# Paged keys taken four pages to a matmul, scores stored by sequence, one more key slot, values loaded onto every fourth partition

## The chip, the core and the metric

The kernel runs on one core of one Trainium2 chip. Five engines work side by side: TensorE (PE, matmuls; its weight loads are listed as PEld), VectorE (DVE), ScalarE (ACT), GpSimd (POOL) and SyncE (SP). SP, POOL and ACT also start DMA transfers, each on a queue of its own, and 16 DMA engines carry them all. SBUF is the on-chip memory of 128 partitions, PSUM holds matmul results in 8 banks of 512 float32 columns. The metric is the device time of one execution in microseconds (us), lower is better.

## What is computed

A decoder step of two layers. 512 prompt tokens and 8 sample tokens (one for each of 8 sequences) go through the same weights. The part that the change touches is the attention of the 8 sample tokens over 4096 cached positions each, held in 32 pages of 128 positions that a page table names:

```python
def mla_sample_attn(q_nope, q_rope, ckv_new, kr_new, ckv_past, kr_past, w_uk, w_uv):
    q_lat = jnp.einsum('bthd,rhd->bthr', q_nope, w_uk)
    s_past = (jnp.einsum('bthr,bsr->bhts', q_lat, ckv_past)
              + jnp.einsum('bthd,bsd->bhts', q_rope, kr_past))
    s_new = (jnp.einsum('bthr,bsr->bhts', q_lat, ckv_new)
             + jnp.einsum('bthd,bsd->bhts', q_rope, kr_new))
    sc = jnp.concatenate([s_past, s_new], axis=-1).astype(jnp.float32) * scale
    pr = jax.nn.softmax(sc, axis=-1)
    o_lat = (jnp.einsum('bhts,bsr->bthr', pr[..., :npast], ckv_past)
             + jnp.einsum('bhts,bsr->bthr', pr[..., npast:], ckv_new))
    o = jnp.einsum('bthr,rhd->bthd', o_lat, w_uv)
```

With 8 heads, 256 latent and 32 rotary columns, a layer reads 256 pages of keys (a transposed copy with 288 columns for each of 128 partitions, 147 KB) and the same 256 pages as values (131 KB). Around it stand the projection `h @ w_in`, the prompt's own attention, a gating MLP, a gated linear attention, and a SwiGLU block, all as matmuls over 520 columns.

## The kernel before

Every weight matrix comes in slabs of 128 output columns (512 KB for 8 blocks of contraction). ACT starts the load and makes a rounded copy `wh`, DVE the rest `wl`, and PE runs three passes (lines 1921 to 1923: high by high, low by high, high by low) for each block and each half of 260 columns. `linear` does one slab: 48 matmuls. PE has one order, written out by hand; what it has to wait for are semaphores of the other engines and of the DMAs.

The sample attention is woven into that order. In each layer there is a **key stage** and then a **value stage**.

- Key stage. 8 pages (2 for each of 4 sequences) are a unit `w`, 32 units a layer. `keys(w)` waits for the unit's load, then takes for each of 4 sequences `bj` a stationary block of 32 query columns (`qlz`), out to 32 PSUM partitions of its own: 8 matmuls of 256 columns for the latent part (line 2177) and 16 of 64 columns for the rotary part (line 2182). Four of them, for four `bj`, run side by side in strips of 32 array columns. Each unit is put between the blocks ("steps") of 12 projection slabs, `KEY_FILLERS`: after 2 or 3 of the 8 steps of each. After the second slab stands `turn_values` (16 transposes), after the fourth `mix_tokens` (64 matmuls, line 2233, from the tile `vtok`). Every bank of 4 units is copied to `scs` by ACT and its maximum taken by DVE. Two sets of 8 head rows of a sequence group (`g`) share the 32 partitions, and of the 32 rows 16 are used.
- Key slots. Five slots: `kpg0` to `kpg2`, the pair `kx_most`/`kx_last`, and `ky`. SP loads the even units, POOL the odd ones, 8 DMAs each, in order. A queue waits until the unit that held the slot is read ("read K.."). Lines 2549 to 2572 (SP) and 2632 to 2643 (POOL).
- Between the stages. DVE makes the maximum of all, ACT the exponentials (line 1675, 8 pieces of 512 columns), PE turns each piece (`turn_scores`, four 128x128 transposes of `scs`) and DVE copies it to `pT`.
- Value stage. 64 value units `u` of 4 pages. `values(col)` waits for two units and does 8 matmuls of 256 columns (line 2207). Each round `c` of 8 has 8 units, a slab `P1c` (4 steps) and a slab `g1(c+1)` (8 steps). Eleven slots `vpg`, later nine; SP and POOL load them by turns, 4 DMAs each (lines 2579 and 2650), each partition taking 1 KB of a page.

## Time and profile before

| | us |
|---|---|
| median of 3 runs | 2041.92 (2040.01 to 2042.92) |
| the profiled execution, its own time | 2037.94 |
| its span in the trace | 2036.2 |
| PE busy | 2017.8 |
| key stage of layer 0 on PE | 173.1 to 302.4 |
| value stage of layer 0 on PE | 311 to 421 |

The profiled execution is 4.0 us below the median of the runs, and 1.7 us of its time lie outside the span. A profile's row of a matmul group is read as: start, length, engine, line, output from inputs, contraction rows * output columns, moving partitions x columns, how many. A float32 matmul is recorded as two instructions, so that `x16` at line 2177 is 8 matmuls. Matmuls overlap; what one costs is read from the starts around it and not from its length. The DMA share of a window is the busy share of the 16 DMA engines; it reads a little over 1 when they are full.

### The profile page before, as it was taken

How to read it: one execution, taken by the hardware profiler on the slowest of the kernel's cores; microseconds unless marked ns; L12 is line 12 of the kernel's file. 1: busy time of each engine (PE TensorE's matmuls, PEld its weight loads, DVE VectorE, ACT ScalarE, POOL GpSimd, SP SyncE). 2: the span in 40 equal slices, each digit the busy share in tenths (PEclk: the TensorE clock that was granted, in tenths of full speed). 3: DMA queues.
4: the chain of work that ended last, by engine and by line, in shares of the span. 5: the costliest groups of instructions: out<-in, count | busy, mean ns of one | idle time of the engine just before them, and what ended most of it. 6: DMA issues, size and time to landing. Idle time of an engine off the chain costs nothing.

```text
span 2036.2 us, 49885 instructions
## 1 busy us (share of the span) xinstructions
PE 2017.8 (99%) x21040; PEld 1915.6 (94%) x21040; DVE 1045.8 (51%) x1605; ACT 716.4 (35%) x1127; POOL 279.1 (14%) x520
## 2 busy tenths in 40 slices
PE   9999999999999999999999999999999999999998
PEld 9998888889999999999999988888999999999998
DVE  7876423366656444433367754234775654444333
ACT  5454114265333222222234531323653332222221
POOL 0003555600000000000000044565000000000000
PEclk9999999999999999999999999999999999999999
DMA  6427899942433333233353298999224333332332
GB/s 230 130 72 263 296 357 325 361 131 67 139 99 95 94 91 93 87 96 87 99 179 105 84 307 299 335 341 364 83 69 131 104 94 94 91 96 86 95 90 75
DMA packets 165557, 322.44 MB, mean 158 GB/s; under 512 B 24419, under 2 KB 104854, under 8 KB 164822
## 3 DMA queue, kind: packets, MB, share of 16 engines
q10 hardware_dynamic: 46944, 147.87, 23.5%
q1 hardware_dynamic: 93814, 100.04, 14.9%
q0 software_dynamic: 24576, 71.34, 10.1%
q8 instruction: 166, 2.72, 0.5%
q14 instruction: 57, 0.47, 0.1%
HBM read 307.08 MB, written 12.08 MB: 157 GB/s over the span
## 4 chain that ended last, share of the span: by engine, by line
PE 95%; DVE 2%; ACT 1%; DMA 1%; issue 0%; ACTq 0%; SPq 0%; DVEq 0%
PE PS L1921 28%; PE PS L1923 27%; PE PS L1922 27%; PE PS L2177 3%; PE PS L2207 3%; PE PS L1974 2%; PE PS L2182 1%; DMA vpg<-in_cache_vals 1%; PE PS L2233 0%; PE PS L2375 0%; PE PS L1960 0%; DVE wl L699 0%; PE PS L1981 0%; PE PS L2337 0%; DVE kxl L706 0%
## 5 line engine op out<-in xcount | busy, mean ns | idle before, releaser
L1921 PE MATMUL PS<-hh,wh 128*128 128x260 f32 x3008 | 862.6, 287 | 1.3 <-DVE gtmp L1104 1.0
L1923 PE MATMUL PS<-hl,wh 128*128 128x260 f32 x3008 | 850.6, 283 | 0.0
L1922 PE MATMUL PS<-hh,wl 128*128 128x260 f32 x3008 | 849.5, 282 | 0.0
L1921 PEld LDWEIGHTS PS<-hh,wh 128*128 128x128 f32 x3008 | 567.2, 189 | 14.9 <-issue 7.1
L1923 PEld LDWEIGHTS PS<-hl,wh 128*128 128x128 f32 x3008 | 567.4, 189 | 0.0
L1922 PEld LDWEIGHTS PS<-hh,wl 128*128 128x128 f32 x3008 | 567.0, 189 | 0.3
L699 DVE TENSOR_TENSOR wl<-raw,wh 128x1024 fp32r<-128x1024 f32 (+4 forms) x326 | 351.0, 1078 | 303.9 <-ACT wh L1455 302.9
L1455 ACT ACTIVATE wh<-raw 128x1024 fp32r<-128x1024 f32 (+4 forms) x326 | 304.3, 937 | 485.2 <-PE PS L1923 478.2
L1921 PE MATMUL PS<-fh,wh 128*128 128x260 f32 x704 | 199.3, 283 | 0.0
L1923 PE MATMUL PS<-fl,wh 128*128 128x260 f32 x704 | 198.7, 282 | 0.0
L1922 PE MATMUL PS<-fh,wl 128*128 128x260 f32 x704 | 198.6, 282 | 0.0
L2650 POOL DMA_DIRECT2D vpg<-in_cache_vals x256 | 137.4, 537 | 86.7 <-PE PS L2207 56.2
L1922 PEld LDWEIGHTS PS<-fh,wl 128*128 128x128 f32 x704 | 132.6, 188 | 0.1
L1923 PEld LDWEIGHTS PS<-fl,wh 128*128 128x128 f32 x704 | 132.6, 188 | 0.0
L1921 PEld LDWEIGHTS PS<-fh,wh 128*128 128x128 f32 x704 | 132.4, 188 | 0.1
L1654 ACT ACTIVATE gsig<-gsig 128x520 f32<-128x520 f32 x48 | 30.6, 638 | 221.0 <-DVE gsig L1095 220.9
L1388 DVE TENSOR_TENSOR fsig<-PS,rs 128x520 f32<-128x520 f32 x44 | 30.8, 700 | 135.5 <-PE PS L1923 135.3
L2622 POOL DMA_DIRECT2D kx_most<-in_cache_keys x14 | 7.6, 546 | 654.4 <-issue 653.5
L1879 ACT ACTIVATE fsig<-fsig 128x520 f32<-128x520 f32 x44 | 28.2, 640 | 196.3 <-DVE fsig L1388 196.2
L2641 POOL DMA_DIRECT2D kpg<-in_cache_keys x112 | 60.1, 537 | 268.4 <-issue 214.8
L1095 DVE TENSOR_TENSOR gsig<-PS,rs 128x520 f32<-128x520 f32 x48 | 33.6, 699 | 122.1 <-PE PS L1923 121.1
L1923 PE MATMUL PS<-ml,wh 128*128 128x260 f32 x256 | 72.3, 283 | 0.0
(362 smaller groups left out, 2989.5 us busy)
## 6 DMA issues: line engine op xcount, KB each, us to landing
raw<-in_wpack ACTq DMA_DIRECT2D x238, 512.0 KB, 3.6
vpg<-in_cache_vals SPq DMA_DIRECT2D x256, 128.0 KB, 6.1
vpg<-in_cache_vals POOLq DMA_DIRECT2D x256, 128.0 KB, 5.4
kpg<-in_cache_keys SPq DMA_DIRECT2D x224, 144.0 KB, 4.5
kpg<-in_cache_keys POOLq DMA_DIRECT2D x112, 144.0 KB, 4.8
ky<-in_cache_keys POOLq DMA_DIRECT2D x96, 144.0 KB, 4.1
raw<-in_wpack ACTq DMA_DIRECT2D x48, 256.0 KB, 2.9
raw<-in_wpack ACTq DMA_DIRECT2D x16, 384.0 KB, 3.1
```

Source lines behind the costliest of these rows:

```text
L699: dve.tensor_tensor(wl[s][:, 0:n], raw[s][:, 0:n], wh[k % W_RING][:, 0:n].bitcast(F32), ALU.subtract).then_inc(*mark("w_low_ready", f"wlo ...
L1095: dve.tensor_tensor(halves(gsig[m % 2][:, :]), pair(f"g{j}{m}"), halves(rs[:, :]), ALU.mult).then_inc(*mark("gate_scaled", f"gate {j}{m}"))
L1388: dve.tensor_tensor(halves(fsig[f % 2][:, :]), pair(f"gt{f}"), halves(rs[:, :]), ALU.mult).then_inc(*mark("gate_scaled", f"scaled {f}"))
L1455: act.activation(wh[k % W_RING][:, 0:n], raw[k % RAW_RING][:, 0:n], ACT.Copy).then_inc(*mark("w_high_ready", f"whi {k}"))
L1921: pe.matmul(out, w[0], x[0], start=first, stop=False)
L1922: pe.matmul(out, w[1], x[0], start=False, stop=False)
L1923: return pe.matmul(out, w[0], x[1], start=False, stop=last)
L1974: return pe.transpose(out, in_, ident[0:n, 0:n])
L2177: ins = pe.matmul(out[32 * bj:32 * bj + 32, q, :], qlz[:, kk, 120 * g + 32 * bj:120 * g + 32 * bj + 32], pages[:, :, PAGE * kk:PAGE * kk + ...
L2207: ins = pe.matmul(bank("O")[r, 256 * g:256 * g + 256], pT[c % 2][:, col % 4, r], vpg[VALUE_SLOT[u]][:, bj, :], start=False, stop=u == 63)
L2641: pool.dma_start(key_page(w, bj, q), a["cache_keys"][bass.ds(l, 1), bass.ds(numbers[4 * q + bj], 1), :, :].rearrange("a n p c -> p (a n c) ...
L2650: pool.dma_start(vpg[VALUE_SLOT[u]][:, bj, :], a["cache_vals"][bass.ds(l, 1), bass.ds(numbers[4 * q + bj], 1), :, :].rearrange("a n p r -> ...
```

## The change

The pages' positions are dealt out otherwise. In the host's copy of the keys, position `4t+j` of a page stands at column `32j+t` of the latent part, and the rotary part is stacked the same way on 4 groups of 32 partitions. A query block now sits in rows `8j..8j+7` of the 32 output rows, with zeros around it, so that position class `j` lands in its own rows: `latent_query(kk, b, j)` is a window of 32 columns moved by 8 for each `j`. All 32 rows of a sequence are used, the rotary part needs one matmul instead of four (`qrz`), and scores are stored by sequence, block and head.

- Two units of one sequence group are taken together in 16 blocks `b` (`KEY_STEP` puts one after every 6 or 7 steps). Where their two slots form one of three `KEY_PAIRS`, one matmul covers 4 pages, 4 x 32 columns: 36 matmuls of 128 columns for two units. Blocks 4 to 15 are such pairs. In blocks 0 to 3 each unit has its own 36 matmuls of 64 columns. Out goes to PSUM with the 32 positions 4 float32 apart.
- Slots: 0, 1, 2, 4, 5, 6 in pairs (1,2), (0,4), (6,5), and slot 3 once. Slot 6 lies over `vtok` and waits for "pe mx3", the end of `mix_tokens`; slot 5 waits for "pe o7".
- `scs` is half as wide (2048 columns in all): 4 pieces to turn instead of 8. The maximum and the sum now have to be taken over four groups of rows as well (`over_blocks`: five small DVE instructions, each waiting for the one before).
- Values: a page goes onto partitions `page, page+4, ...` of a slot, 32 partitions with 4 KB each instead of 128 with 1 KB. A group is 4 slots, waited for together, then 16 matmuls of 256 columns with 8 stationary columns each. 13 slots, later 11.
- The new tokens' part has four matmuls more, `Ot` two transposes more, and tiles of the linear attention (`S1`, `zz`, `ATd`, `hv1`, `hr1`) lie elsewhere; DVE's `head_variances` waits for "out S1 1".

```diff
-KEY_SLOT = [4, 3, 0, 1, 2, 4, 0, 3, 1, 2, 4, 3] + [0, 1, 2, 4] * 5
+KEY_STEP = {round(6.4 * b) - 1: b for b in range(1, 16)}
+KEY_BANKS = ((0, 2), (2, 6), (6, 10), (10, 14), (14, 16))
+KEY_SLOT = [4, 3, 0, 1, 2, 0, 4, 5] + [1, 0, 2, 4, 6, 1, 5, 2, 0, 6, 4, 5, 1, 0, 2, 4, 6, 1, 5, 2, 0, 6, 4, 5]
+KEY_PAIRS = ((1, 2), (0, 4), (6, 5))
...
-                            for q, pages in key_pages(w, bj):
-                                ins = pe.matmul(out[32 * bj:32 * bj + 32, q, :], qlz[:, kk, 120 * g + 32 * bj:120 * g + 32 * bj + 32],
-                                                pages[:, :, PAGE * kk:PAGE * kk + PAGE], start=(g, kk) == (0, 0), stop=False)
...
+                    out = bank(f"K{n}")[:, at:at + 128].rearrange("p (t i q) -> p i q t", i=2, q=2)
+                    blocks = [(kk, j) for kk in range(2) for j in range(4)] + [(2, 0)]
...
+                        for w in units:
+                            pe.wait_ge(*upto(f"keys {w}"))
+                        for kk, j in blocks:
+                            x = slice(PAGE * kk + 32 * j, PAGE * kk + 32 * j + 32)
+                            for bj in range(4):
+                                ins = pe.matmul(out[32 * bj:32 * bj + 32, :, :, :], stationary(kk, j, bj), key_pair[slots][:, :, bj, :, x],
+                                                start=(kk, j) == (0, 0), stop=kk == 2)
...
+                def over_blocks(src, op):
+                    dve.tensor_reduce(by_row[:, 0:2], src, AX.X, op).then_inc(*mark("dve_step"))
...
+                    dve.transpose(turned_rows[:, :], by_row[:, :]).then_inc(*mark("dve_step"))
...
+                    dve.tensor_reduce(best[:, :], turned_rows[:, :].rearrange("p (j h) -> p h j", j=4), AX.X, op).then_inc(*mark("dve_step"))
...
+                    dve.tensor_copy(spread[:, :, :], best[:, :].unsqueeze(1).broadcast_to([128, 4, 8])).then_inc(*mark("dve_step"))
...
+                    dve.transpose(by_row[:, :], spread[:, :, :].rearrange("p j h -> p (j h)")).then_inc(*mark("dve_step"))
...
+                    elif KEY_SLOT[w] == 6:
+                        sp.wait_ge(*upto("pe mx3"))
...
-                            sp.dma_start(vpg[VALUE_SLOT[u]][:, bj, :],
-                                         a["cache_vals"][bass.ds(l, 1), bass.ds(numbers[4 * q + bj], 1), :, :].rearrange("a n p r -> p (a n r)")).then_inc(
+                            for page in range(4):
+                                sp.dma_start(vpg[VALUE_SLOT[u]][page:128:4, :, :].rearrange("t j r -> t (j r)"),
+                                             a["cache_vals"][bass.ds(l, 1), bass.ds(numbers[page // 2][2 * (page % 2) + bj], 1), :, :].rearrange("a n (t j) r -> t (a n j r)", j=4)).then_inc(
```

On PE, the first key unit behind `mix_tokens` of layer 0, before (`kpg_141` is slot 0; rows between are the slab's passes):

```order
L2233 MATMUL PS<-wsT,vtok 64x128 x7
L1921 MATMUL PS<-hh,wh_63 128x260 [waits w_low_ready,dve_evac]
...
L1923 MATMUL PS<-hl,wh_63 128x260
L2177 MATMUL PS<-kpg_141,qlz 32x256 [waits keys_loaded0,act_evac]
L2177 MATMUL PS<-kpg_141,qlz 32x256 x7
L2182 MATMUL PS<-kpg_141,qlz 32x2x32 x16
L1921 MATMUL PS<-hh,wh_63 128x260
```

and with the change (`kp_215` are slots 0 and 4, `kp_216` slots 6 and 5):

```order
L2243 MATMUL PS<-kp_215,qlz 32x4x32 [waits keys_too_loaded4,keys_too_loaded0]
L2243 MATMUL PS<-kp_215,qlz 32x4x32 x31
L2243 MATMUL PS<-kp_215,qrz 32x4x32 x4
L2311 MATMUL PS<-wsT,vtok 64x128 [waits dve_evac,value_ready]
...
L2311 MATMUL PS<-wsT,vtok 64x128 x7
L1975 MATMUL PS<-hh,wh_63 128x260 [waits w_low_ready,dve_evac]
...
L1977 MATMUL PS<-hl,wh_63 128x260
L2243 MATMUL PS<-kp_216,qlz 32x4x32 [waits keys_loaded5,keys_loaded6,low_ready]
L2243 MATMUL PS<-kp_216,qlz 32x4x32 x31
L2243 MATMUL PS<-kp_216,qrz 32x4x32 x4
```

24 matmuls for one unit, behind 8 steps, became 36 for two units, behind 6 steps, and they wait for both loads, into slots 6 and 5.

On SP, the same unit pair's loads, units 12 and 14, before (`kpg0_141` slot 0; between the shown rows of a unit stand its other DMAs):

```order
L2572 DMA out_new_gmlp_v_sample<-xT_49 512x1x8 [waits value_ready]
L680 TENSOR_LOAD ptab_79
L2567 ISA [waits keys_read]
L2567 DMA kpg0_141<-in_cache_keys 128x288
...
L680 TENSOR_LOAD ptab_79
L2567 ISA [waits keys_read]
L2567 DMA kpg2_143<-in_cache_keys 128x288
```

and with the change:

```order
L2654 DMA out_new_gmlp_v_sample<-xT_49 512x1x8 [waits value_ready]
L706 TENSOR_LOAD ptab_79
L2649 ISA [waits group_ready]
L2649 DMA kp65_216<-in_cache_keys 128x288
...
L706 TENSOR_LOAD ptab_79
L2649 ISA [waits keys_read]
L2649 DMA kp65_216<-in_cache_keys 128x288
```

The wait ahead of unit 12 is no longer for a key unit that PE has read but for a group of PE, which is "pe mx3"; the loads of unit 14 and all later even units are queued behind it.

## Rows read from the trace of the kernel before

**Rows 1.** The page: busy time by engine, and the DMA share in 40 slices.
```profile
PE 2017.8 (99%) x21040; PEld 1915.6 (94%) x21040; DVE 1045.8 (51%) x1605; ACT 716.4 (35%) x1127; POOL 279.1 (14%) x520
...
DMA  6427899942433333233353298999224333332332
```

**Rows 2.** Busy time of windows of layer 0; last PE clock, DMA share, GB/s.
```profile
200.00:210.00 10.00, 10.00 (x166) 9.26 (x165) 5.87 (x8) 1.66 (x2) 4.29 (x8) 1.00 1.05 349
...
220.00:230.00 10.00, 10.00 (x144) 9.25 (x141) 9.51 (x17) 2.64 (x4) 1.51 (x3) 1.00 0.53 189
...
250.00:260.00 10.00, 10.00 (x189) 8.28 (x188) 2.61 (x3) 1.66 (x2) 5.83 (x12) 1.00 1.06 369
...
310.00:320.00 10.00, 10.00 (x114) 6.87 (x114) 2.28 (x3) 9.91 (x19) 4.49 (x9) 1.00 0.67 225
...
330.00:340.00 10.00, 10.00 (x112) 8.42 (x114) 3.17 (x4) 1.57 (x2) 6.45 (x12) 1.00 1.06 390
...
400.00:410.00 10.00, 8.03 (x84) 6.71 (x80) 4.23 (x9) 3.47 (x4) 4.30 (x9) 1.00 1.05 369
```

**Rows 3.** Timeline of PE around one key unit of layer 0.
```profile
180.66 0.28 PE L1923 MATMUL PS<-hl,wh 128*128 128x260 f32 x1
180.87 1.07 PE L2177 MATMUL PS<-kpg,qlz 128*32 128x256 f32 x16
181.76 0.63 PE L2182 MATMUL PS<-kpg,qlz 128*32 128x64 f32 x32
182.32 0.39 PE L1921 MATMUL PS<-hh,wh 128*128 128x260 f32 x1
182.55 0.28 PE L1922 MATMUL PS<-hh,wl 128*128 128x260 f32 x1
```

**Rows 4.** Groups of PE by line and shape: count, busy us, mean ns, idle before.
```profile
L2207 PE MATMUL PS<-vpg,pT 128*32 128x256 f32 x1024 | 62.7, 382 | 2.2 <-DMA vpg<-in_cache_vals 2.2
L2177 PE MATMUL PS<-kpg,qlz 128*32 128x256 f32 x672 | 45.0, 385 | 0.0
...
L2182 PE MATMUL PS<-kpg,qlz 128*32 128x64 f32 x1344 | 26.5, 219 | 0.0
...
L1974 PE MATMUL PS<-ident,scs 128*128 128x128 f32 x64 | 9.7, 274 | 0.0
```

**Rows 5.** Timeline of PE at the end of the value stage of layer 0.
```profile
399.81 1.07 PE L2207 MATMUL PS<-vpg,pT 128*32 128x256 f32 x16 [0.18 <-DMA vpg<-in_cache_vals]
...
409.79 1.07 PE L2207 MATMUL PS<-vpg,pT 128*32 128x256 f32 x16 [1.97 <-DMA vpg<-in_cache_vals]
```

**Rows 6.** Key loads: a unit's issue on SP and POOL, SP's waits, landing (150 to 215).
```profile
182.59 3.95 SPq L2567 DMA_DIRECT2D kpg<-in_cache_keys  x8
...
191.38 4.66 POOL L2641 DMA_DIRECT2D kpg<-in_cache_keys  x8 [5.29 <-PE PS L2182]
...
SPq L2567 <- PE PS L2182: 94.6, 22, 12.2
...
DMA to landing us min/median/max: 3.1/5.1/8.1
```

**Rows 7.** The chain that ended last: `mix_tokens`, start, length, line.
```profile
219.14 4.47 PE PS L2233 x64
```

**Rows 8.** Timeline between the stages of layer 0: maximum, exponentials, first turned piece.
```profile
303.14 0.69 DVE L1034 TENSOR_REDUCE mxs<-scs 128x1 f32<-128x512 f32 x1 [10.18 <-ACT scs L1649]
...
304.54 0.16 DVE L1086 TENSOR_REDUCE nms<-mxs 128x1 f32<-128x9 f32 x1
...
306.72 0.71 ACT L1675 ACTIVATE scs<-scs,nms 128x512 f32<-128x512 f32 x1
...
308.43 0.60 PE L1974 MATMUL PS<-ident,scs 128*128 128x128 f32 x4
```

**Rows 9.** Windows of 2 us in which the granted clock of TensorE fell.
```profile
168.00:170.00 2.00, 2.00 (x10) 2.00 (x9) 1.85 (x8) 0.00 (x0) 0.00 (x0) 0.50 1.03 319
...
1448.00:1450.00 2.00, 2.00 (x12) 1.93 (x11) 1.97 (x7) 0.27 (x1) 0.00 (x0) 0.50 0.37 115
```

More of the change, by code:

```diff
@@ L2236, in mix_tokens @@
                         ins.then_inc(*mark("group_ready", f"pe mx{i}"))
-                for unit in range(KEYS_FIRST):
-                    keys(unit)
+                keys(0)
                 pv(7)
```

382 lines of the change are left out of this document (222 added, 160 removed).

## The prediction, made before the changed kernel was run

> **What bounds the kernel now.** I read the page first: PE is busy for 2017.8 of 2036.2 us [rows 1], so time is lost or won where PE's own work or a wait of PE changes, and DVE (51%) and ACT (35%) matter only where PE waits for them. The DMA share by slices [rows 1] is the second thing to see: it is 2 to 4 tenths nearly everywhere, but 7 to 9 in two stretches of five slices, which are the key and value stages of the two layers. The windows of layer 0 make this sharp [rows 2]: from 180 to 410 us the 16 DMA engines are full (share 1.05, 349 to 390 GB/s), except for three dips, of which the deepest is 220 to 230 (0.53), where PE does `mix_tokens` and frees no key slot, and another is 310 to 320 (0.67). PE is not idle there, but the loads are only just in time: at the end of the value stage PE waits 0.18 and 1.97 us for a value load [rows 5]. SP for its part waits 94.6 us in 22 waits for PE to read key units [rows 6]. So in these stages PE and the DMA engines run at nearly the same pace. If PE gets faster there, the loads become the limit. The expected gain has to be taken as the smaller of two differences.
>
> **Part 1, key matmuls (less PE work).** A unit of before [rows 3]: PE's last pass ahead of it starts at 180.66, the second behind it at 182.55. Without the unit that would take 2 x 0.12 us (the distance of passes), so a unit costs 1.65 us; 0.89 us are the 16 records of 256 columns, 0.56 us the 32 records of 64 columns, 0.2 us the change of shape on both sides. 32 units are 52.8 us a layer. By columns: four records side by side take 222 ns for 256 columns and 70 ns for 64. The changed pair has 72 records of 128 columns, 18 groups of four. Half of 222 ns is 111 ns; from the short shape up, 70 ns plus 64 columns at 222/256 ns is 126 ns. I take 117, so 2.1 us and with the 0.2 us 2.3 us for two units. The 8 units of blocks 0 to 3 have 72 records of 64 columns: 18 x 70 ns = 1.26 us each. Sum: 12 x 2.3 + 8 x 1.26 + 4 x 0.2 + 0.3 for the split slot 3 = 38.8 us. This is **14.0 us less a layer**, all of it on PE's path.
>
> No matmul of before writes PSUM with gaps; the changed ones put neighbouring positions 4 float32 apart. So the price of 117 ns has no row behind this side. Bounds: no effect below (a write can't become faster by gaps), and above twice the group's time, that is, each gapped record of 128 columns costing what 256 columns cost without gaps (222 ns). I take no effect, since a group of four with 256 columns needs 222 ns, or 0.87 ns for one column, about two periods of a 2.4 GHz clock, so that a write has two periods already.
> The Trainium skill speaks against this change here: its page "Advanced Engine Details and Errata", section "PSUM Cachelines", says that PSUM has cachelines of 8 bytes and that any non-contiguous access pattern slows matmuls significantly. No row of before can show it. By that rule the gain of part 1 turns into a loss, which is rival B below.
>
> **Part 2, fewer turns.** 64 transposes of `scs` in both layers cost about 0.6 us for four [rows 4, 8], 4 groups a layer go: 2.4 us. Against it stand one more transpose of `sn8`, two of `Oacc` and four matmuls of 256 columns, 0.8 us together. **1.6 us less a layer.** The values' matmuls keep their number and columns, 512 a layer at 62.7 us of 1024 records in all [rows 4]; 8 stationary columns instead of 32 I cost at nothing (their strips of 32 are the same; bounds minus 1 us a layer, if a part of the 9 ns above the plain column time is weight load, and nothing above).
>
> Parts 1 and 2: 15.6 us of PE work less in each layer.
>
> **Part 3, the wait of block 6 (new).** Units 12 and 14 go to slots 6 and 5, and unit 12 waits for "pe mx3". Before, 5 slots cycled and the load of unit 12 waited only for an earlier unit. Now SP can start it when `mix_tokens` ends (219.14 + 4.47 = 223.6 us in before [rows 7]). SP needs 3.95 us for 8 DMAs [rows 6], twice plus 0.3 us for page numbers, and a DMA takes at least 3.1 us from its issue to landing [rows 6]: the second unit is there 0.3 + 3.95 + 0.35 + 3.6 + 3.1 = 11.1 us after mx3 (the last DMA is issued 0.4 us before the end). Block 6 stands 6 steps (6 x 0.717 = 4.3 us) behind `mix_tokens`. **PE waits 6.5 us, in each layer.** All of PE's order is behind it, and on SP the loads of all later even units are queued behind the "mx3" wait. This wait can't be hidden, since nothing on PE stands between. POOL has units 13, 15 and 17 issued by then, but its unit 19 waits for slot 6.
>
> **Part 4, loads behind block 6.** A pair takes 6.4 steps (4.6 us) and 2.3 us, 6.9 us. In that time 2 x 1.18 MB of keys and 0.8 of a slab (0.42 MB) have to come: 403 GB/s, against 349 to 369 in full windows of the key stage [rows 2]. At 355 GB/s a pair needs 7.8 us. From block 6 to block 15 there are 9 periods, 8.4 us of waits if nothing is loaded ahead; 3 units are, and by bytes alone (15 units and 7 slabs, 21.4 MB, 60.3 us, plus 3 us landing, against 62.3 us of PE) 1 us is left. Between 1 and 8.4: going through the stage unit by unit with these lengths, slots and the two queues, I get 5.8 us at 355 GB/s and 4.9 at 360. The same tally for before has no wait in the key stage, 1.0 us in the value stage, and its end at 421.6, where the trace shows 421. **I take 5.5 us a layer.** In the value stage, PE's round needs 4.98 MB in about 13 us in both kernels; 13 slots and later 11 instead of 11 and 9 cover it, so the 2.2 us of layer 0 [rows 5] go.
>
> **Part 5, small things between the stages.** Maximum, `nms` and exponentials end just ahead of PE: the first piece is done at 307.5 and turned at 308.43 [rows 8], 0.9 us of cover. `over_blocks` adds four dependent instructions of 0.19 us on DVE, ACT has two pieces for each one (plus 0.9 us), the last bank is half as wide (minus 0.6): 1.1 to 1.2 us, so 0.3 us on PE a layer. The `over_blocks` behind the value stage runs while PE turns the values and does D0 and D1 (3 us), at nothing. `head_variances` waits for a store that is some 30 us old.
>
> **Part 6, value loads.** Same bytes and number of DMAs, 4 KB rows instead of 1 KB. Rows of 4 KB (the weight slabs) and of 1 KB run mixed in the full windows, so no row tells their rates apart; bounds 340 to 410 around the 355 to 390 there [rows 2]. Faster than now gives nothing (part 4), so I take the present rate.
>
> **Sum.** A layer: -15.6 + 6.5 + 5.5 + 0.3 = -3.3 us; two layers -6.6, less the 2.2 of rows 5: -8.8. A fall of TensorE's clock during the new 6.5 us wait is likely in one layer or the other: at 0.50, that is 1.2 GHz, PE started 10 or 12 matmuls in 2 us [rows 9] where the passes' distance of 0.12 us gives 17; such a window loses 0.7 us or so and its neighbours a part more. Ahead of it PE had run small matmuls only. I add 1.5. Total -7.3 us: the profiled execution 2037.94 becomes 2030.6, the median 2041.92 becomes **2034.5**.
>
> **The rivals.**
> A, the loads keep up. For: in the windows at 250 and 330, 369 and 390 GB/s were moved. Then part 4 gives nothing back and only block 6 is waited for: 2 x (-15.6 + 6.5 + 0.3) - 2.2 = -19.8, about **2022**.
> B, slower: PSUM writes with gaps double a group. It decides once a group of 128 columns takes more than about 150 ns. At 213 ns a pair costs 4.0 us, an alone unit 1.95: 65.2 us against 52.8, +12.4 a layer, -1.6, +6.5 for block 6, +0.3, part 4 gone, -2.2 once: +33, **2075**. Against it: the two periods for a column, above. The skill's rule speaks for it.
> C, slower: rows on every fourth partition come in worse, 320 GB/s in the value stage. A round then needs 15.6 us against 13; with 13 slots ahead, 6 rounds wait, about 11 us a layer: -8.8 + 22 + 1.5, **2056**. Against: the four loads of a slot cover all partitions together.
> D, no change: the change does its work, but the waits take it all (355 GB/s turns out 345, part 4 8 us; both block-6 waits drop the clock): -15.6 + 7 + 8 + 0.3 is -0.3 a layer, -2.2, +3: **2041**.
> That the matmuls with 8 stationary columns would not run four side by side (the change not doing what it says) would be over +80 us a layer; every float32 strip of 32 in before does, so 1%.
>
> **How the numbers follow.** Forecast 0.41, A 0.15, B 0.14, C 0.08, D 0.21, the last 0.01. A measurement here tells 0.2%, 4 us, from no change. Faster by more: A, and most (0.35) of the forecast: 0.50. Same: the rest of it and most of D: 0.24. Slower: B, C, the last, some of D: 0.26. The range reaches from below A (2017) to beyond C (2060), leaving out B and the best end of A.
>
> **What would show it.** Key matmuls: line 2243 groups, four records 117 ns apart (right) or over 150 (B). Part 3: PE idle some 6.5 us, released by a key DMA, once a layer behind `mix_tokens`, DMA share low there. Part 4: waits of 1 to 2 us for key loads at blocks 10 to 15 with DMA share near 1.05; none would be A. Part 6: value-stage GB/s of 355 or more, no waits at value groups. Wrong altogether if PE waits for DVE or ACT between the stages by more than 1 us.

## The result, and the profile of the changed kernel

The changed kernel takes 2059.51 us, median of 4 runs (2055.8 to 2060.82), against 2041.34 for the kernel before on the same chip: a ratio of 1.0087, 95% interval 1.0073 to 1.0100. It is **slower**, by 18 us. The forecast was 2034.5 and faster; the range of 2017 to 2060 holds the time, near its upper end. The profiled execution is 2055.8 us against 2037.94, its span 2054.1 against 2036.2, so the two traces differ by 17.9 us.

The page answers [rows 1]: PE's busy time, and the DMA share in 40 slices.

```profile
span 2054.1 us, 49473 instructions
...
PE 1998.5 (97%) x20802; PEld 1915.3 (93%) x20802; DVE 1039.3 (51%) x1611; ACT 709.6 (35%) x1125; POOL 274.1 (13%) x520
...
DMA  6427899942432323333353289999324323333332
```

PE is busy for 19.3 us less than before, and its idle time grew from 18.4 to 55.6 us. What PE waited for (line, releaser, us in total, times, longest):

```profile
PE PS L2243 <- DMA kp<-in_cache_keys: 26.1, 6, 8.7
PE PS L2253 <- issue: 9.8, 3, 4.4
```

L2243 is a key pair, L2253 an unpaired key unit. The waits of [rows 5] for values have no line any more. The groups that answer [rows 4]:

```profile
L2284 PE MATMUL PS<-vpg,pT 128*8 128x256 f32 x1024 | 61.2, 380 | 0.0
L2243 PE MATMUL PS<-kp,qlz 128*32 128x128 f32 x1536 | 53.7, 298 | 26.3 <-DMA kp<-in_cache_keys 26.1
...
L2028 PE MATMUL PS<-ident,scs 128*128 128x128 f32 x32 | 4.9, 276 | 0.0
```

The timeline of PE in layer 0, key stage and after, tells where the time went (start, length, operation, idle time ahead and its releaser; it answers [rows 3], [rows 7] and [rows 8]):

```profile
173.67 1.10 PE L2253 MATMUL PS<-kp,qlz 128*32 128x64 f32 x64
...
191.72 1.08 PE L2253 MATMUL PS<-kp,qlz 128*32 128x64 f32 x64
197.20 0.44 PE L2253 MATMUL PS<-kp,qrz 128*32 128x64 f32 x8 [4.41 <-issue]
...
221.38 1.96 PE L2243 MATMUL PS<-kp,qlz 128*32 128x128 f32 x64 [1.44 <-DMA kp<-in_cache_keys]
...
223.48 4.54 PE L2311 MATMUL PS<-wsT,vtok 128*64 128x128 f32 x64
...
241.18 3.64 PE L2243 MATMUL PS<-kp,qlz 128*32 128x128 f32 x64 [8.66 <-DMA kp<-in_cache_keys]
244.56 0.68 PE L2243 MATMUL PS<-kp,qrz 128*32 128x128 f32 x8
...
275.72 3.64 PE L2243 MATMUL PS<-kp,qlz 128*32 128x128 f32 x64 [4.09 <-DMA kp<-in_cache_keys]
...
314.27 0.40 PE L2243 MATMUL PS<-kp,qrz 128*32 128x128 f32 x8
...
320.77 0.60 PE L2028 MATMUL PS<-ident,scs 128*128 128x128 f32 x4
...
325.48 1.91 PE L2284 MATMUL PS<-vpg,pT 128*8 128x256 f32 x32
...
432.79 0.66 PE L2028 MATMUL PS<-ident,Oacc 128*128 128x128 f32 x4
```

Three things can be seen. Block 6 (241.18) waits as foretold, and longer; block 10 (275.72) waits too. The wait at 197.20 is one that the prediction had not: it stands **inside** a unit, ahead of its last 8 records, where the program has no wait at all. And the same 64 records that take 1.96 us at 221.38 take 3.64 behind the long waits, since TensorE's granted clock had fallen to 0.50, that is 1.2 of 2.4 GHz. The windows show both that and the DMA engines (PE, PEld, DVE, ACT, POOL, granted clock, DMA share, GB/s), against [rows 2] and [rows 9]:

```profile
200.00:210.00 10.00, 10.00 (x203) 9.77 (x203) 4.19 (x4) 1.59 (x2) 2.09 (x4) 0.89 0.29 81
...
240.00:250.00 10.00, 8.82 (x107) 8.47 (x108) 1.93 (x2) 1.06 (x1) 3.47 (x7) 0.67 0.92 268
...
340.00:350.00 10.00, 10.00 (x102) 8.77 (x99) 2.83 (x5) 1.24 (x2) 7.38 (x15) 1.00 1.02 398
...
238.00:240.00 2.00, 0.00 (x0) 0.00 (x0) 0.00 (x0) 0.00 (x0) 0.00 (x0) 0.50 0.83 245
244.00:246.00 2.00, 2.00 (x28) 1.62 (x21) 0.00 (x0) 0.00 (x0) 0.09 (x1) 0.50 0.83 240
```

From 200 to 210 the share was 1.05 before [rows 2]; now it is 0.29, with PE at work all the time. The queues say why. GpSimd's queue, SyncE's queue, and what SyncE's waited for in this layer (they answer [rows 6]):

```profile
182.23 4.97 POOL L2726 DMA_DIRECT2D kp<-in_cache_keys  x8 [0.66 <-issue]
207.76 2.30 POOL L2726 DMA_DIRECT2D kp<-in_cache_keys  x4 [20.56 <-PE PS L2253]
```
```profile
185.72 11.89 SPq L2649 DMA_DIRECT2D kp<-in_cache_keys  x16
197.66 0.60 SPq L2654 DMA_DIRECT2D out_new_gmlp_v_sample<-xT  x1
228.20 42.29 SPq L2649 DMA_DIRECT2D kp<-in_cache_keys  x53
```
```profile
SPq L2649 <- PE PS L2311: 29.2, 1, 29.2
```

GpSimd's queue stood 20.6 us with unit 9, whose slot 0 still held unit 5 (read only in block 3, at 207), though slot 4, for unit 11 behind it, was free from 197.6 on. SyncE's stood 29.2 us with unit 12, for the end of `mix_tokens` at 228.0, though slot 5 for unit 14 was free from block 3 on.

Time from start to start, in both traces. The key stage runs from its first to the end of its last key matmul, the value stage from its first value matmul (325.48) to the first transpose of `Oacc` (432.79). Half clock is the busy time of PE in windows of 1 us, times what the granted clock there lacks to 1.

| | predicted, a layer | layer 0 | layer 1 |
|---|---|---|---|
| key stage before | | 173.1 to 302.4, 129.3 | 1180.7 to 1310.1, 129.4 |
| key stage after | | 173.7 to 314.7, 141.0 | 1188.8 to 1328.1, 139.3 |
| of it: waits inside units | 0 | 4.4 | 5.4 |
| of it: wait of block 5 | 0 | 1.4 | 1.3 |
| of it: wait of block 6 | 6.5 | 8.7 | 7.6 |
| of it: waits behind block 6 | 5.5 | 4.1 | 3.1 |
| of it: half clock | 1.5 in both | 7.6 | 7.2 |
| the rest, PE's own work | -14.0 | 114.8, so -14.5 | 114.8, so -14.6 |
| between the stages | +0.3 | +0.6 | +0.6 |
| value stage | -1.6, and -2.2 once | 112.3 to 107.3, -5.0 | 109.7 to 107.3, -2.4 |

Unrounded, the sums are +7.2 and +8.1 us; the other 2.6 of the 17.9 us lie outside these stages. Over the whole program half clock takes 18.0 us in this trace and 5.1 in the trace of before, 12.9 us more. PE's longer idle time (+37.2) and its shorter work apart from the clock (-32.2) leave the other 5.0.

### The profile page after: what moved, and what is told of

The parts are those of the page before. It is cut to its first block, busy times and chain, and to the rows that moved or that the text cites. A ratio compares the mean times of both kernels' runs of the same rounds, so it can differ in the third digit from the quotient of the medians.

```text
span 2054.1 us, 49473 instructions
## 1 busy us (share of the span) xinstructions
PE 1998.5 (97%) x20802; PEld 1915.3 (93%) x20802; DVE 1039.3 (51%) x1611; ACT 709.6 (35%) x1125; POOL 274.1 (13%) x520
## 3 DMA queue, kind: packets, MB, share of 16 engines
q8 instruction: 164, 2.69, 0.5%
## 4 chain that ended last, share of the span: by engine, by line
PE 90%; DMA 3%; issue 2%; SPq 2%; DVE 2%; ACT 1%; POOLq 0%; ACTq 0%; POOL 0%; DVEq 0%
PE PS L1975 27%; PE PS L1977 26%; PE PS L1976 26%; PE PS L2284 3%; DMA kp<-in_cache_keys 2%; PE PS L2243 2%; SPq L2649 2%; PE PS L2028 2%; PE PS L2253 1%; PE PS L2311 0%; PE PS L2415 0%; PE PS L2453 0%; PE PS L2014 0%; DMA xT<-in_x_t 0%; PE PS L2035 0%
## 5 line engine op out<-in xcount | busy, mean ns | idle before, releaser
L2726 POOL DMA_DIRECT2D kp<-in_cache_keys x240 | 129.7, 540 | 362.1 <-issue 232.7
L2736 POOL DMA_DIRECT2D vpg<-in_cache_vals x256 | 131.8, 515 | 88.5 <-PE PS L2284 50.3
L2243 PE MATMUL PS<-kp,qlz 128*32 128x128 f32 x1536 | 53.7, 298 | 26.3 <-DMA kp<-in_cache_keys 26.1
```

The source lines that it names most:

```text
L2243: ins = pe.matmul(out[32 * bj:32 * bj + 32, :, :, :], stationary(kk, j, bj), key_pair[slots][:, :, bj, :, x], start=(kk, j) == (0, 0), sto ...
L2726: pool.dma_start(key_page(w, bj, q), a["cache_keys"][bass.ds(l, 1), bass.ds(numbers[number_of(bj, q)], 1), :, :].rearrange("a n p c -> p ( ...
L2736: pool.dma_start(vpg[VALUE_SLOT[u]][page:128:4, :, :].rearrange("t j r -> t (j r)"), a["cache_vals"][bass.ds(l, 1), bass.ds(numbers[page / ...
```

## The experiments

All times are medians, each beside runs of the kernel before on the same chip (2038.8 to 2041.7 us). The changed kernel's variants scatter more than the kernel before (2045.6 to 2058.0 in e5, 2031.3 to 2056.3 in e14), so a difference between two of them is clear only where their intervals lie apart. The changed kernel's own is 1.0073 to 1.0100. The theory at the start: what is lost is waits for key loads, and the half clock behind them, on PE's path. The first question was what makes the loads late: the slot behind `mix_tokens`, the order of the queues, or the rate of the DMA engines (called L below).

**Block 6 in free slots.**

```diff
-KEY_SLOT = [...] + [1, 0, 2, 4, 6, 1, 5, 2, 0, 6, 4, 5, ...
+KEY_SLOT = [...] + [1, 0, 2, 4, 1, 0, 2, 4, 6, 0, 5, 4, ...
```


> One edit of the changed kernel: block 6 takes slots 1 and 2 (free when block 4 is read), block 7 slots 0 and 4, block 8 slots 6 and 5, block 9 slots 0 and 4. No load ahead of block 6 waits for mix_tokens any more. Theory W (the wait at block 6 is the slot over vtok, with the half clock behind it): the idle time of 8.7 and 7.6 us at block 6 goes or falls under 2 us, and with it the half clock of some 5 us behind it (2.2 us of work lost); loads run on through mix_tokens, so the wait of 4.1 and 3.1 us at block 10 shrinks too. Per layer 7 + 2.2 + 2, so 2059.5 - 22 = about 2037. Rival L (the DMA engines' rate sets the end of the stage): the wait only moves from block 6 to blocks 8 to 13, total of waits falls by no more than 3 us a layer, 2050 to 2057.

Measured 2061.54, ratio 1.0107 (1.009 to 1.0124), no gain. Block 6 waited no more, but PE waited for keys 25.2 us in 8 waits. Block 5 waited longer, 3.1 and 4.2 us in place of 1.4 and 1.3. The longest waits stand at block 9, which takes slots 0 and 4 two blocks after block 7 had them, and has to wait until they are read and loaded:

```profile
261.95 3.64 PE L2243 MATMUL PS<-kp,qlz 128*32 128x128 f32 x64 [5.13 <-DMA kp<-in_cache_keys]
```

So the wait of block 6 can't be taken away by itself. As a test between slots and rate it was poor, since the edit made a new slot shortage.

**Work that keeps PE busy while it waits.**

```diff
                     if b == first:
                         begin(f"K{n}")
+                        for i in range({6: 18, 10: 6}.get(b, 0)):
+                            for bj in range(4):
+                                pe.matmul(bank(f"K{n}")[32 * bj:32 * bj + 32, 0:256], latent_query(0, bj, 0), qlz[:, 0, 0:256], start=True, stop=True)
```
The first run had 36 and 14 in place of 18 and 6.

> The changed kernel with matmuls that do nothing needed ahead of block 6 (36 groups of four with 256 columns, some 8 us at full clock) and ahead of block 10 (14 groups, some 3 us), written into the bank that the block then overwrites. PE would have been idle there. It prices TensorE's clock by itself. Theory C (the half clock behind each wait costs its 2.2 to 2.5 us of work and PE's time is the path): granted clock stays at 1.00 behind blocks 6 and 10, the waits are as long as the filler leaves, and the time falls by 2 x (2.2 + 2.3) = 9 us, to 2050.5; less where the filler itself runs over the end of the wait. Rival L (loads set the pace): what the clock gives is waited for at the next blocks, within 2 us of 2059.5.

Measured 2069.14, ratio 1.0151 (1.0132 to 1.0169): the filler was twice as long as meant, 15.6 us, and block 6 came at 246.8 in place of 241.2. It tells nothing of the clock's price. The second run was sized by it:

> The filler again, half as long: 18 groups (144 records) ahead of block 6 and 6 groups ahead of block 10. In the run before, 288 records took 15.6 us, 54 ns each, and PE came to block 6 at 246.8 in place of 241.2: I had counted a matmul as one record, it is two. Now 7.8 and 2.6 us. Theory C (half clock costs its 2.3 us behind each wait, on the path): clock 1.00 behind blocks 6 and 10, key stage ends 4 us earlier in each layer, 2059.5 - 8 = 2051. Rival L (loads set the pace): the waits at blocks 10 and 15 grow by what the clock gives, within 3 us of 2059.5.

Measured 2055.91, ratio 1.0075 (1.0058 to 1.0092): 3.6 us less than the changed kernel, where theory C said 8 and L said 3 or less. The intervals overlap, so these 3.6 us are not clear. The clock stayed at 1.00 behind blocks 6 and 10 of both layers, but blocks 8 and 14 of layer 0 then waited 2.7 and 2.1 us and block 8 of layer 1 3.2 us; block 14 ran at half clock, and that block 8 in part:

```profile
255.24 1.96 PE L2246 MATMUL PS<-kp,qlz 128*32 128x128 f32 x64 [2.69 <-DMA kp<-in_cache_keys]
...
301.87 3.43 PE L2246 MATMUL PS<-kp,qlz 128*32 128x128 f32 x64 [2.14 <-DMA kp<-in_cache_keys]
```

The falls of the clock only moved: the half clock of both layers, from 140 to 480 and from 1150 to 1500, adds up to 17.5 us here and to 18.0 in the changed kernel. Two of the falls in this trace (315 to 320 and 1332 to 1337) have no wait for a load near them. So the run doesn't price the clock by itself, and keeping it up at single waits brought nothing back here.

**PSUM without gaps**, the price that no row of before could show.

```diff
-out = bank(f"K{n}")[:, at:at + 128].rearrange("p (t i q) -> p i q t", i=2, q=2)
+out = bank(f"K{n}")[:, at:at + 128].rearrange("p (i q t) -> p i q t", i=2, q=2)
```


> The key matmuls of the changed kernel write their 32 positions side by side in PSUM (no gaps of 4 float32) in place of one in four; the scores then stand in another order than the values' turning expects, nothing else changes. Theory (gaps cost nothing): a pair's 64 latent records stay at 1.95 us (111 ns for a group of four), the unpaired ones at 1.10, and the time is the same within 0.2%. Rival (gaps slow the write): the 64 records fall below 1.7 us and the time by 2 x 12 x 0.3 = 7 us or more.

Measured 2057.12, ratio 1.0087 (1.0067 to 1.0107), the same as the changed kernel's. The 64 records at full clock take as long as with gaps (1.96 above):

```profile
247.92 1.95 PE L2243 MATMUL PS<-kp,qlz 128*32 128x128 f32 x64
```

Rival B is out.

**Small key loads, in the changed kernel and in the kernel before.**

```diff
-sp.dma_start(key_page(w, bj, q),
+sp.dma_start(key_page(w, bj, q)[:, 0:KCOL if KEY_HOLDER[w] is None else 72],
```
and likewise for the source and for GpSimd's loads.

> The changed kernel with the same number of key DMAs, but only the first load of each slot is whole; later ones bring 72 of the 288 columns, a quarter of the bytes (scores of later units are then partly those of earlier ones). It takes the DMA engines' rate out and leaves queues, slots, landing and PE's work. Theory (rate and slots together): waits at blocks 5, 10 and the waits inside units without a semaphore (4.4, 3.0, 2.4 us, when a 16 KB block of PE's instructions came in beside full DMA engines) go, block 6 still waits, some 4 to 7 us with its half clock, since its loads start at the end of mix_tokens: 2059.5 - 38 - 15 + 2 x 8 = about 2022. If the waits inside units stay at 3 to 4 us, they have nothing to do with the load of the DMA engines: 2032. Rival (PE's work has not shrunk as read): over 2040.

Measured 2031.36, ratio 0.9956 (0.994 to 0.9971), 28 us less than the changed kernel (37 expected). Its waits:

```profile
PE PS L2243 <- DMA kp<-in_cache_keys: 14.1, 4, 6.9
PE PS L2253 <- issue: 2.7, 2, 1.4
```

Block 6 still waits 6.9 and 6.3 us, as a load behind `mix_tokens` must; the waits inside units fell from 9.8 to 2.7 us (two of 1.4 and 1.3), with the same instructions at the same places.

> The kernel before with later key loads of 72 of 288 columns (scores of later units are then partly those of earlier ones), as in e4 for the changed kernel, which fell by 28 us. Theory: the kernel before waits for no key load, so it stays within 3 us of its time, 2038 to 2041. Rival (full DMA engines slow something else too, such as PE's instructions or its matmuls): below 2033.

Measured 2040.87, ratio 1.0004 (0.9992 to 1.0017), as the theory said: small loads by themselves made that kernel no faster.

**Two unpaired units apart**, against the waits inside units.

```diff
-                keys(0)
+                keys(0, 0)
                 pv(7)
+                keys(0, 1)
...
+                        if KEY_STEP.get(8 * n + k - 2, 9) < 4:
+                            keys(KEY_STEP[8 * n + k - 2], 1)
```


> The changed kernel with the two unpaired units of blocks 0 to 3 apart: the second unit of block 0 behind the prompt's last matmuls, those of blocks 1 to 3 two steps after the first. Same matmuls, same loads. Theory I (a block of two unpaired units is 144 records and as many weight loads, 288 instructions in 2 us, and PE's next 16 KB of instructions comes in late beside full DMA engines): the waits of 3 to 4.4 us inside a unit, where the program has no wait, go or fall under 1.5 us, with the half clock behind them; 2059.5 - 2 x (3.5 + 2) = 2048 if nothing is waited for later, 2055 if half of it is. Rival U (it is the key load of the unit, put down wrongly): the waits stay, at the start of the second unit, 2058 to 2061.

Measured 2050.24, ratio 1.0064 (1.0039 to 1.0089): 9.3 us less than the changed kernel by the medians, though the intervals overlap. The trace decides: no wait inside a unit is left; the lines of PE's waits for keys and of its longest wait under "issue" are

```profile
PE PS L2243 <- DMA kp<-in_cache_keys: 29.0, 6, 8.6
PE PS L2423 <- issue: 1.2, 1, 1.2
```

(29.0 with the keys where it was 26.1: a part was given back at block 10.) So U falls. What these waits are can be seen in the DMA queues of the changed kernel:

```profile
q8 instruction: 164, 2.69, 0.5%
```

164 transfers of 16 KB are 2.69 MB. Their number follows PE's records: 154 for 19468 matmul records and as many weight loads in e12 and e15, 166 for 21040 in the kernel before, 171 for 21602 in e2, always 253 or 254 instructions of PE to a transfer. So this is PE's program coming in. In the stretch 194 to 196, just ahead of the end of the wait at 197.20, one such transfer is listed, while key loads held 99% of the engines:

```profile
q1 hardware_dynamic: 658, 0.67, 99.2%
q8 instruction: 1, 0.02, 3.5%
```

The waits of layer 1 look the same:

```profile
1193.76 0.32 PE L2253 MATMUL PS<-kp,qlz 128*32 128x64 f32 x8 [2.98 <-issue]
1214.20 0.48 PE L2253 MATMUL PS<-kp,qlz 128*32 128x64 f32 x19 [2.44 <-issue]
```

Windows of 0.1 us place the transfers that belong to the three waits at 194.6, 1191.1 and 1211.8; PE goes on 2.6, 2.7 and 2.4 us later. That distance is the same wherever such a wait occurs: in all 33 waits of this kind, 0.7 to 4.4 us long, in twelve traces of the changed kernel and its variants, PE goes on 2.3 to 2.7 us after one transfer on this queue has started, also in e4 (2.5 and 2.7), where the waits are short. Blocks of two unpaired units are 288 instructions in 2 us, more than one transfer brings. The Trainium skill, "Runtime: NRT & Kernel Launch", section "Instruction fetch mechanics", has it that an engine's instructions come in blocks of 16 KB, 256 instructions, while it works, and that this is mostly hidden; the size agrees with the trace, the hiding doesn't hold here. The runs show when the wait goes (units apart) or shrinks (small loads), and the fixed distance from the transfer speaks strongly for the instruction supply as the cause; why the transfer starts late beside full DMA engines is not shown. In e7, e10, e11, e14 and e16, whose units are apart too, waits of 0.7 to 2.9 us inside a unit came back, so apart is not enough by itself.

**The order of the queues.**

```diff
-KEY_SLOT = [4, 3, 0, 1, 2, 0, 4, 5]
+KEY_SLOT = [4, 3, 0, 1, 2, 3, 4, 5]
...
-                for w in range(3, 32, 2):
+                for w in (3, 9, 7, 5, *range(11, 32, 2)):
...
-                for i in range(16):
+                for i in (*range(6), 7, 6, *range(8, 16)):
```


> The changed kernel with other orders on the two load queues: unit 5 goes to slot 3 (read once before, then empty), unit 9 is loaded ahead of 7 and 5 into slot 0, and unit 14 (slot 5) ahead of unit 12 (slot 6, behind mix_tokens). Theory Q (queues that stand for a slot while others are empty cost the time: GpSimd's queue stood 20.6 us, SyncE's 29.2 us in layer 0, and the DMA share fell to 0.29 from 200 to 210): the share at 200 to 240 rises to over 0.95, the wait at block 6 falls from 8.7 to 4 to 5 us (one unit behind mix_tokens in place of two), block 5 waits no more, block 10 waits under 2 us. Per layer 4 + 1.4 + 2 and one half clock less (2.3): 2059.5 - 19 = about 2040. Rival L (rate): less than 6 us in all, over 2053.

Measured 2051.21, ratio 1.0054 (1.0035 to 1.0073): 8.3 us less, between Q (19) and L (under 6). Waits for key loads fell from 26.1 to 11.9 us, but 5.4 us more of block 6 are listed under "issue" (it starts 7.3 us behind the end of `mix_tokens`, with unit 12's load), and the waits inside units stayed (9.9 us). The share from 200 to 210 rose from 0.29 to 0.69, not to 0.95.

> Both edits together. Theory: they add up where neither hides the other, 2059.5 - 19 - 8 = 2032, below the kernel before. If the loads' rate is the limit, it comes out as the better of the two, not lower.

Measured 2046.83, ratio 1.0028 (1.0013 to 1.0044): 12.7 us less than the changed kernel, better than either by the medians, but not the 27 of the sum. Block 8 now waits 4.0 and 6.4 us, for units 16 and 18.

Two more orders on that line missed. Unit 16 ahead of unit 12:

```diff
-                for i in (*range(6), 7, 6, *range(8, 16)):
+                for i in (*range(6), 7, 8, 6, *range(9, 16)):
```


> As e7, and unit 16 is loaded ahead of unit 12 as well (SyncE's queue: 10, 14, 16, 12, 18). In e7 block 8 waited 4.0 and 6.4 us for units 16 and 18, queued behind the load of unit 12 that waits for mix_tokens. Theory Q: unit 18 is issued 4 us earlier, the wait of block 8 falls to 0 to 2.5 us and its half clock goes in one layer at least: 2046.8 - 2 x 4 = 2039. Rival L (rate): half of it or less, 2043 or more.

Measured 2048.35, ratio 1.0046 (1.0026 to 1.0067). Block 6 itself waited 5.6 us in both layers in place of 3.2 and 2.6, with unit 16's load issued ahead of its own; block 8 waited no more. And other steps besides:

```diff
-KEY_STEP = {round(6.4 * b) - 1: b for b in range(1, 16)}
+KEY_STEP = {s: b + 1 for b, s in enumerate((4, 10, 17, 24, 30, 40, 46, 52, 58, 64, 71, 77, 83, 89, 95))}
```


> As e10, with the blocks at other steps: 1 to 5 after steps 4, 10, 17, 24, 30 (one or two steps earlier, slots come free sooner), block 6 after step 40 in place of 37 (2.2 us later, unit 12 lands some 7.4 us behind mix_tokens), the rest every 6 or 7 steps. Theory: the hole in the DMA share from 200 to 240 gets smaller, block 6 waits under 1.5 us, 3 to 5 us less than e10 in all, about 2036. Rival L: the rate sets it, same as e10 within 2 us.

Measured 2051.39, ratio 1.0063 (1.0039 to 1.0086), 15 us above the theory; block 6 waited 3.7 and 3.4 us, block 10 of layer 0 5.8. Both results spoke for L, that the rate is the limit, until e12 and e15 below.

**Without waits: PE's own work.** e4, e1 and e5 together.

> The changed kernel with nothing to wait for in the key stage as far as that can be had: later key loads bring 72 of 288 columns (as in e4; scores of later units are then partly those of earlier ones), block 6 takes free slots (as in e1), unpaired units stand apart (as in e5). It measures the term of the sum by itself: PE's work. Theory (parts 1 and 2 of the prediction right, 15.6 us a layer): 2041 - 31 = 2010, a little less since the unpaired units took 1.03 us in place of 1.26 (8 x 0.2 x 2 = 3): 2005 to 2012, waits under 3 us a layer. Rival (the gain was never there, the traces' waits only show it): over 2025.

Measured 2020.78, ratio 0.9905 (0.9876 to 0.9934): 20 us below the kernel before, where 31 were expected. The key stage of layer 0 runs from 174.0 to 293.5, 119.5 us with 2.7 us of waits, so 12.5 us of work less; units apart may cost some of the 14.5, with more changes of shape.

**One part alone, in the kernel before: two units at once.**

```diff
-KEY_STEPS = [(2, 5, 7) if n % 2 == 1 else (3, 7) for n in range(len(KEY_FILLERS))]
+PAIR_AT = [round(6.4 * b) - 1 for b in range(1, 16)]
+KEY_STEPS = [tuple(s % 8 for s in PAIR_AT if s // 8 == n for _ in range(2)) for n in range(len(KEY_FILLERS))]
...
                             keys(KEY_START[n] + KEY_STEPS[n].index(k))
+                            keys(KEY_START[n] + KEY_STEPS[n].index(k) + 1)
```


> The kernel before with one part of the change alone: two key units at once after every 6 or 7 steps (the changed kernel's places) in place of one after 2 or 3 steps; its own matmuls, slots and value stage. Theory G (taking two units at once frees slots in pairs and later, so that the load queues stand and the DMA engines have holes): PE waits for key loads, 3 to 8 us a layer, 2047 to 2060. Rival (the grain does nothing, only the faster PE and slot 6 do): within 3 us of 2040.

Measured 2035.87 (10 runs), ratio 0.9978 (0.9968 to 0.9987). Theory G falls, on the other side: this is **faster** than the kernel before, with one wait of 0.5 us for keys. The timeline shows what is won. Two units and the pass behind them:

```profile
190.48 0.28 PE L1924 MATMUL PS<-hl,wh 128*128 128x260 f32 x1
190.70 1.07 PE L2178 MATMUL PS<-kpg,qlz 128*32 128x256 f32 x16
191.58 0.63 PE L2183 MATMUL PS<-kpg,qlz 128*32 128x64 f32 x32
192.03 1.05 PE L2178 MATMUL PS<-ky,qlz 128*32 128x256 f32 x16
192.89 0.63 PE L2183 MATMUL PS<-ky,qlz 128*32 128x64 f32 x32
193.45 0.39 PE L1922 MATMUL PS<-hh,wh 128*128 128x260 f32 x1
193.68 0.29 PE L1923 MATMUL PS<-hh,wl 128*128 128x260 f32 x1
```

From 190.48 to 193.68 less two passes of 0.12 us are 2.96 us for two units, against 2 x 1.65 by [rows 3]: one change of shape less. The key stage of layer 0 is 173.5 to 298.6, 4.2 us shorter.

**Is it the pace?** The kernel before with three of four rotary matmuls left out, unit by unit, then two at once:

```diff
-                    for t in range(4):
+                    for t in range(1):
```


> The kernel before with three of four rotary key matmuls left out (8 of 24 instructions' groups stay: scores lack part of the rotary product). PE's work in the key stage shrinks by 24 records of 64 columns a unit, 0.42 us, 13.4 us a layer: about what the change takes away, but with one unit at a time, the slots of before and no load behind mix_tokens. Theory L (the loads of the key stage stand so near PE's pace that any faster PE runs into them): the DMA share of that stage was 0.95, so some 6 us a layer are to be had and the rest turns into waits with half clock behind them; 2041 - 2 x 7 = 2027. Rival S (only the slots and order of the change spoil it): all of it shows, 2014. Rival N: nothing is to be had at all, over 2036.

Measured 2025.55, ratio 0.9924 (0.9903 to 0.9945), close to the value of L; but I had sized the removed work too large. By the distance of unit to unit it is 0.3 to 0.35 us a unit, some 10 us a layer, and of these the key stages got 9.0 and 9.9 us shorter (173.9 to 294.2 in layer 0, 120.3 us). PE waited little for keys:

```profile
PE PS L2177 <- DMA kpg<-in_cache_keys: 2.4, 2, 1.7
```

The DMA engines were full where the changed kernel's stood (200 to 210: share 1.06, 374 GB/s). So in the key stages nearly all of the work saved shows, as S has it. The whole program got less of it, 14.6 us by the medians and 11.4 in the profiled execution: that trace has 11.7 us of half clock in five places, none behind a wait for keys, against 5.1 in the trace of before. Why the clock fell there is open.

> The kernel before with two units at once (e9, its key stage 125 us) and without three of four rotary matmuls (e12, 120 us): with both PE's key stage is about 115 us, the pace of the changed kernel, with five slots, unit by unit releases and no load behind mix_tokens. Theory S: waits up to 4 us a layer, 2035.9 - 15 + 3 = about 2024 or less. Rival L: PE waits 6 us or more a layer with half clock behind it, key stage no shorter than the 120 us of e12, 2028 or more.

Measured 2023.56, ratio 0.992 (0.9902 to 0.9938). The key stages are 118.3 and 117.3 us, with 5.9 us of waits for keys in both layers together, so PE goes nearly at the changed kernel's own pace (114.8):

```profile
200.00:210.00 10.00, 10.00 (x125) 9.04 (x117) 4.96 (x7) 1.66 (x2) 6.46 (x12) 1.00 1.07 381
210.00:220.00 10.00, 10.00 (x147) 9.31 (x146) 4.84 (x8) 2.19 (x3) 6.47 (x12) 1.00 1.07 362
```

So the load engines do feed nearly this pace, from five slots in the order of before.

**The changed kernel with a cycle of three slot pairs**, on top of e7: units apart, unit 5 in slot 3 and unit 9 early are in it too, besides what is shown, and the waits of the value slots follow their new order.

```diff
-KEY_SLOT = [...] + [1, 0, 2, 4, 6, 1, 5, 2, 0, 6, 4, 5, 1, 0, 2, 4, 6, 1, 5, 2, 0, 6, 4, 5]
+KEY_SLOT = [...] + [1, 0, 2, 4, 1, 0, 2, 4, 6, 1, 5, 2, 0, 6, 4, 5, 1, 0, 2, 4, 6, 1, 5, 2]
...
-FIRST_SLOTS, LATER_SLOTS = (4, 5, 6, 1, 2, 3, 11, 12, 10, 9, 7, 8, 0), (4, 5, 6, 1, 2, 3, 11, 12, 7, 8, 0)
+FIRST_SLOTS, LATER_SLOTS = (1, 2, 11, 12, 8, 9, 10, 3, 4, 5, 6, 7, 0), (2, 11, 12, 8, 1, 3, 4, 5, 6, 7, 0)
...
-                for i in range(16):
+                for i in (*range(6), 9, 6, 7, 8, *range(10, 16)):
```


> The changed kernel with its load order set anew: unpaired units apart (e5), unit 5 in slot 3 and unit 9 early (e6), and from block 4 on the slot pairs (1,2), (0,4), then (1,2), (0,4), (6,5), (1,2), (0,4), (6,5) and so on, so that block 6 needs no load behind mix_tokens (as in e1) and no pair is taken again sooner than three blocks later, but for blocks 6 and 7 (in e1 block 9 was, and waited 5.1 us); unit 18 goes to slot 5 ahead of unit 12. The value slots are taken in the order in which the key slots now come free. Theory S (slots and order of the change spoil it, since in e12 the same load engines fed a key stage of 120 us with waits of 1 to 2 us): waits of the key stage under 5 us a layer and one half clock at most, key stage 120 to 125 us, 2059.5 - 2 x 16 = about 2027. Rival L (the last 5 us of pace are more than the loads can do): key stage 130 or more as in e7 and e10, 2043 to 2048.

Measured 2042.13 (10 runs), ratio 1.0002 (0.9978 to 1.0027): level with the kernel before, 17.4 us less than the changed kernel. The key stages are 127.6 and 131.4 us, more than the 120 to 125 expected, with waits of 8.6 and 11.4 us. The last run put the queues right for the units that were late there:

```diff
-                for w in (3, 9, 7, 5, *range(11, 32, 2)):
+                for w in (3, 7, 5, 9, 11, 18, *range(13, 32, 2)):
...
-                for i in (*range(6), 9, 6, 7, 8, *range(10, 16)):
+                for i in (*range(9), *range(10, 16)):
```


> As e14, with the early loads in another order: GpSimd's queue takes units 3, 7, 5, 9, 11, 18 and then 13 on (unit 5 is no longer behind 9: block 3 waited 2.0 and 2.3 us for it), and unit 18 moves from SyncE's queue to GpSimd's, which stood 18.9 us for unit 13's slot while SyncE was behind with units 20 and 22 (block 10 waited 4.0 and 4.5 us). Theory S: block 3 waits no more, block 10 waits under 2 us and keeps its clock, 2042 - 2 x 4.5 = about 2033. Rival L (in 230 to 270 the DMA share is full, so the order there changes nothing): block 10 waits as long, 2038 to 2042.

Measured 2037.95 (12 runs), ratio 0.9987 (0.9975 to 0.9998): 21.6 us less than the changed kernel, and barely faster than the one before. The interval overlaps with that of e14, and S had 2033, L 2038 to 2042: by the time, L is nearer. Block 3 waits under 1 us; block 10 still waits 3.8 us in layer 0 and 2.3 in layer 1, where S had under 2 and L no change from 4.0 and 4.5:

```profile
PE PS L2243 <- DMA kp<-in_cache_keys: 9.7, 6, 3.7
PE PS L2255 <- issue: 5.1, 4, 2.6
```

## Why the prediction was wrong, step by step

- **Part 1, key matmuls: right.** A pair costs 2.31 us (last pass ahead at 250.78, second pass behind at 253.33, less two passes of 0.12), where 2.3 was predicted. Four records of a pair are 1.77 us / 16, 111 ns, the lower of my two values. The unpaired unit took 1.03 us, not 1.26: its 64 records start within 0.92 us, 57 ns for four where I took 70. With that unit the sum would be 15.8 us a layer; PE's own work fell by 14.5 and 14.6, where 14.0 was predicted.
- **PSUM gaps: right, no effect** (e3, 1.95 against 1.96 us). The rule that the prediction quotes from the Trainium skill, "Advanced Engine Details and Errata", section "PSUM Cachelines", is not borne out for these float32 matmuls.
- **Part 2 and rows 5: right in size.** The value stage is 5.0 and 2.4 us shorter; 3.8 and 1.6 were predicted.
- **Part 3, block 6: the mechanism right, the term too small.** 8.7 and 7.6 us against 6.5. The prediction's own terms add up to 11.3 and not 11.1, and less 4.3 to 7.0. From the end of `mix_tokens` to block 6 it was 13.2 us in layer 0 and 12.1 in layer 1. The issue was slower than assumed: SyncE took 12.00 us for 19 DMAs, so some 10 us for the 16 of block 6, where twice 3.95 was taken:

```profile
228.20 12.00 SPq L2649 DMA_DIRECT2D kp<-in_cache_keys  x19
```

- **Part 4, behind block 6: too large**, 4.1 and 3.1 us against 5.5. Part 5 was small, as predicted: +0.6 us a layer against +0.3.
- **The step that failed: the stretch ahead of block 6, put at nothing.** The prediction asked of that part only whether the loads keep up in bytes. It did not follow the queues through blocks 0 to 5: unit 9 waits for a slot that block 3 hands back, and everything on GpSimd's queue is behind it, 20.6 us with the DMA share at 0.29. Waits of 5.9 and 6.7 us stood there, of which 4.4 and 5.4 inside units; the sum had 0 for all of them. The part outside units, 2.7 us, is block 5 waiting for units 9 and 11 of that queue; with the queue in another order (e6) it was under 1 us. The waits inside units, 9.8 us, are PE's own instructions (e5). Such a wait has no row in the trace of before, whose key units are 96 instructions and not 288 at a place. The number of small instructions in one place was a cost of part 1, and the prediction gave it none.
- **The clock: right in kind, too small by a factor of ten, the term most mis-sized.** 1.5 us were added for one fall in one layer; there were three falls in each layer's key stage, which cost 14.8 us in all, 2.5 on average. Each came in or just behind a wait, and four of the six, 10.6 us, at blocks 6 and 10, whose waits the prediction had. How much of it would go with the waits is not shown: e2b kept the clock up at two of the three places, and it fell elsewhere for as long.
- **The sum.** The forecast for the profiled execution was -7.3 us, the measured difference +17.9. Of these 25.2 us, 13.3 are the half clock and 12.5 the waits ahead of block 6. Block 6 (+3.3) and the waits behind it (-3.8) nearly cancel, and PE's own work (-1.1), the value stages (-2.0), the time between the stages (+0.5) and the rest of the program (+2.6) are small. So that the range up to 2060 holds the time is not to the prediction's credit: its upper end was set for rival C, whose cause did not occur.
- **The rivals.** None was what happened. D (the waits take it all, 2041) was nearest in kind; A, B and C fell: loads did not keep up, gaps cost nothing, and the value stage ran at 398 GB/s from 340 to 350 without a wait. The bound "355 GB/s against 403 wanted" was not what held the changed kernel: e12 and e15 fed PE's faster pace at 360 to 380 GB/s with waits of 2.4 and 5.9 us over both layers. What the changed kernel lacked in front of block 6 was free slots early enough, on both queues.

How much is shown: that late key loads and the waits inside units make the loss (e4, e8 with small loads, against e13); that slots, order and units apart are together most of it (e14 and e16, 17 and 22 us, with nearly the same matmuls; units apart alone had 9 by the medians, e5, so 8 to 12 are left for slots and order); that neither the grain of two units (e9) nor the pace (e15) needs to cost more than a few us. Open is what holds block 10 in e16, where the DMA share of 230 to 270 is 0.98 to 1.06: there the rate may be the limit, after a share of 0.83 from 210 to 220. It was not separated.

## What to carry to other kernels

When an engine gets faster in a stage that is fed just in time, a sum of bytes and rate is not enough: write down for each queue, in its order, which slot each load waits for and who hands it back, from the first load of the stage on. A queue that stands for one slot holds back loads whose slots are free, and here the hole in the DMA share came 10 to 30 us ahead of PE's waits. Price each wait with the half clock behind it as well, 2.5 us on average here. Try the cheap part by itself as well: two units at once, without the new layout, gave 5 us (e9).
